# Gated recurrence of a two-block model: scaling at the last level, one rate product for both directions, and where the keys' factor is applied

## The reference

```
q = silu(q_raw);  v = i_in
f = lb + (1 - lb) * sigmoid(f_raw)         # for both directions: (256, 2, 1024)
log_f = log(max(f, 1e-30))
k = (1 - lb) * sigmoid(-f_raw)
o_f = scan(q, k[0], v, log_f[0])           # state = state * f_t + k_t v_t;  o_t = q_t . state
o_b = flip(scan(flip(q), flip(k[1]), flip(v), flip(log_f[1])))
y_hg = group_rmsnorm(o_f + o_b) * silu(g_out)
```

## Time and profile before

| | |
|---|---|
| median of 3 runs | 2481.41 us (2479.23 to 2483.37) |
| profiled execution, its own time | 2486.97 us |
| its span | 2485.1 us |
| PE busy | 2430.2 us, 98% |
| DVE busy | 1787.8 us, 72% |
| ACT busy | 1451.0 us, 58% |
| POOL busy | 287.6 us, 12% |
| mean granted clock of TensorE | 0.995 of full |

### The profile page before, as it was taken

One profiled execution on the slowest core, in us unless ns is written; L12 is line 12 of the kernel. 1 busy time (PEld: TensorE's weight loads), 2 busy tenths in 40 slices (PEclk: granted clock), 3 DMA queues, 4 the chain that ended last, 5 costly groups with the idle time before them and its releaser, 6 DMA issues.

```text
span 2485.1 us, 43110 instructions
## 1 busy us (share of the span) xinstructions
PE 2430.2 (98%) x17744; PEld 2225.9 (90%) x17744; DVE 1787.8 (72%) x2889; ACT 1451.0 (58%) x2130; POOL 287.6 (12%) x222
## 2 busy tenths in 40 slices
PE   8999999999999999899999999999999999999998
PEld 7888999888889899798999799998898999899996
DVE  4558675565586755589778897885599768887875
ACT  5547555545475555477656655664767656556654
POOL 0000002000000000002124710000012207500000
PEclk9999999999999999999999999999999999999999
DMA  7554476655545556554567646565554557645663
GB/s 246 160 141 125 154 253 192 203 181 167 141 119 153 185 189 204 166 159 123 154 189 200 198 134 194 184 190 190 145 159 137 172 173 205 181 151 186 190 209 127
DMA packets 358921, 430.50 MB, mean 173 GB/s; under 512 B 20617, under 2 KB 286311, under 8 KB 358469
## 3 DMA queue, kind: packets, MB, share of 16 engines
q1 hardware_dynamic: 341312, 401.72, 52.9%
q10 hardware_dynamic: 14340, 14.93, 2.7%
q0 software_dynamic: 3072, 11.10, 1.5%
HBM read 424.44 MB, written 3.24 MB: 172 GB/s over the span
## 4 chain that ended last, share of the span: by engine, by line
PE 86%; DVE 10%; ACT 2%; issue 1%; DMA 1%; ACTq 0%; POOL 0%; POOLq 0%; DVEq 0%
PE ps L112 84%; DVE wlo L121 3%; PE ps L115 2%; DVE sE L121 1%; DVE hgA L148 1%; DVE hgQF L121 0%; ACT L118 0%; DVE hgQB L121 0%; ACT lnv L118 0%; DVE hgkf L121 0%; DVE hgkb L121 0%; DMA kT<-in_diff_lambda 0%; DVE sbc L130 0%; DVE sE L124 0%; ACT whi L118 0%
## 5 line engine op out<-in xcount | busy, mean ns | idle before, releaser
L121 DVE TENSOR_TENSOR wlo<-wring,whi 128x1024 fp32r<-128x1024 f32 (+1 forms) x768 | 919.8, 1218 | 252.5 <-ACT whi L118 252.2
L118 ACT ACTIVATE whi<-wring 128x1024 fp32r<-128x1024 f32 (+1 forms) x768 | 803.4, 1054 | 428.3 <-PE ps L112 416.0
L112 PE MATMUL ps<-uT,whi 128*128 128x256 f32 x4640 | 821.7, 281 | 6.0 <-DVE wlo L121 4.7
L112 PEld LDWEIGHTS ps<-uT,whi 128*128 128x128 f32 x4640 | 706.4, 188 | 16.3 <-DVE wlo L121 8.1
L112 PE MATMUL ps<-uT,wlo 128*128 128x256 f32 x2320 | 646.8, 279 | 0.0
L112 PEld LDWEIGHTS ps<-uT,wlo 128*128 128x128 f32 x2320 | 437.5, 189 | 0.0
L112 PE MATMUL ps<-xT,whi 128*128 128x256 f32 x2112 | 375.0, 282 | 2.3 <-DVE xT L121 1.1
L112 PEld LDWEIGHTS ps<-xT,whi 128*128 128x128 f32 x2112 | 320.3, 187 | 9.4 <-issue 5.2
L112 PE MATMUL ps<-xT,wlo 128*128 128x256 f32 x1056 | 293.7, 278 | 0.0
L112 PE MATMUL ps<-whi,hid 128*128 128x512 f32 x864 | 269.5, 391 | 0.0
L112 PEld LDWEIGHTS ps<-xT,wlo 128*128 128x128 f32 x1056 | 197.8, 187 | 0.3
(11 more groups left out here) (400 smaller groups left out, 3565.4 us busy)
## 6 DMA issues: line engine op xcount, KB each, us to landing
wring<-in_w_in SPq DMA_DIRECT2D x346, 512.0 KB, 4.2
wring<-in_mlp_w SPq DMA_DIRECT2D x128, 512.0 KB, 4.5
wring<-in_w_up SPq DMA_DIRECT2D x88, 512.0 KB, 4.6
wring<-in_w_down SPq DMA_DIRECT2D x44, 512.0 KB, 4.3
wring<-in_w_branch SPq DMA_DIRECT2D x32, 512.0 KB, 3.4
wring<-in_w_out SPq DMA_DIRECT2D x32, 512.0 KB, 4.3
wring<-in_mem_w_kv SPq DMA_DIRECT2D x16, 512.0 KB, 6.4
wring<-in_w_br_hg SPq DMA_DIRECT2D x16, 512.0 KB, 4.7
```

The costliest lines, as they stand in the source:

```text
L112: return self.e.matmul(*p, **k) if self.e else Nothing()
L118: return self.e.activation(*p, **k) if self.e else Nothing()
L121: return self.e.tensor_tensor(*p, **k) if self.e else Nothing()
```

## The change

`hg_scale` at level 6 works only on the tokens that `hg_cross` reads: 4 instructions of 256 columns in place of 512. The four rate buffers become one tile `W.T` in which both directions lie 768 columns apart, and f and b become two parts of one 2048-column tile `hgfb`, so that one instruction makes both directions' rates at levels 0 to 5, and `hg_split` is one instruction of 2048 columns in place of two of 1024. In `forget_scale` the maximum is one instruction of 512 columns in place of two of 256, and the two multiplications of the keys move to a new ScalarE part of the same step: two activations of 256 columns with a per-channel scale, in place. `hg_start` and level 0's merge now wait for ScalarE's signal for the keys, and `hg_split` for the maxima.

```diff
@@ -1030,9 +1030,10 @@
                 return out
-            B.f, B.kf = ar.take("hgf", 1024, at=o + 1024), ar.take("hgkf", 1024, at=o + 3072)
+            B.fb, B.kf = ar.take("hgfb", 2048, at=o + 1024), ar.take("hgkf", 1024, at=o + 3072)
+            B.f, B.b = B.fb.part("f", 0, 1024), B.fb.part("b", 1024, 1024)
             yield from projB(w, GF + c0, 512, uT, forget(B.f, B.kf, hf * 4))
-            B.b, B.kb = ar.take("hgb", 1024, at=o + 2048), ar.take("hgkb", 1024, at=o + 4096)
+            B.kb = ar.take("hgkb", 1024, at=o + 4096)
             yield from projB(w, GF + 1024 + c0, 512, uT, forget(B.b, B.kb, 8 + hf * 4))
@@ -1065,9 +1066,9 @@
             do("hg_cross", B, [AB.take(), AB.take()])
-            ar.give(B.q, B.f, B.b, B.kf, B.kb)
+            ar.give(B.q, B.fb, B.kf, B.kb)
             if hf:
-                ar.give(*W.Tf, *W.Tb, *W.QK[1])
+                ar.give(W.T, *W.QK[1])
             yield
@@ -1101,9 +1102,9 @@
             W = Box()
-            W.QF, W.QB, W.At = ar.take("hgQF", 1024, at=8192), ar.take("hgQB", 1024, at=9216), ar.take("hgA", 2048, at=10240)
-            W.Tf = [ar.take("hgTf", 512, at=12288), ar.take("hgTf", 256, at=12800)]
-            W.Tb = [ar.take("hgTb", 512, at=13056), ar.take("hgTb", 256, at=13568)]
+            W.Q2, W.At = ar.take("hgQ", 2048, at=8192), ar.take("hgA", 2048, at=10240)
+            W.QF, W.QB = W.Q2.part("F", 0, 1024), W.Q2.part("B", 1024, 1024)
+            W.T = ar.take("hgT", 1536, at=12288)
             W.QK = [[ar.take("hgQm", 1024, at=13824 + 2048 * i), ar.take("hgKm", 1024, at=14848 + 2048 * i)] for i in range(2)]
@@ -1270,7 +1271,7 @@
             yield from branch(acc, a["w_br_hg_2"][l], 0, yT, gT[1], 0, keep=True)
-            ar.give(gT[1], W.QF, W.QB, W.At)
+            ar.give(gT[1], W.Q2, W.At)
         weave((ssd_proj(), 1), (hg_branch(), 1))
@@ -1951,6 +1952,14 @@
 
+    def forget_scale(c, fk, kk, i0, k):
+        e.wait_ge(*at("bounds"))
+        e.wait_ge(*at((kk.name, "sig", k)))
+        for j in range(2):
+            v = kk.ap[:, (k + j) * 256:(k + j + 1) * 256]
+            o = e.activation(v, v, ACT.Copy, scale=K.oms[:, c.l, i0 + k + j:i0 + k + j + 1])
+        o.then_inc(*up("act_forget", (kk.name, k)))
+
     def halves(x, side, n):
...
@@ -2518,18 +2527,13 @@
         e.wait_ge(*at((fk.name, "sig", k)))
-        fs, ks = ([x.ap[:, (k + j) * 256:(k + j + 1) * 256] for j in range(2)] for x in (fk, kk))
+        fs = fk.ap[:, k * 256:k * 256 + 512]
         lb, om = ([v[:, c.l, i0 + k + j:i0 + k + j + 1] for j in range(2)] for v in (K.lbs, K.oms))
         for j in range(2):
-            o = e.tensor_scalar(fs[j], fs[j], om[j], lb[j], ALU.mult, ALU.add)
+            o = e.tensor_scalar(fs[:, j * 256:j * 256 + 256], fs[:, j * 256:j * 256 + 256], om[j], lb[j], ALU.mult, ALU.add)
         o.then_inc(*up("dve_forget"))
         e.wait_ge(*now("dve_forget"))
-        for j in range(2):
-            e.tensor_scalar(fs[j], fs[j], TINY, None, ALU.max)
-        e.wait_ge(*at((kk.name, "sig", k)))
-        for j in range(2):
-            o = e.tensor_scalar(ks[j], ks[j], om[j], None, ALU.mult)
-        o.then_inc(*up("dve_forget", (kk.name, k)))
+        e.tensor_scalar(fs, fs, TINY, None, ALU.max).then_inc(*up("dve_forget", (fk.name, k)))
 
@@ -2554,23 +2558,34 @@
             e.wait_ge(*at((B.q.name, k)))
-        e.tensor_tensor(W.QF.ap, B.q.ap, B.f.ap, ALU.mult)
-        e.tensor_tensor(W.QB.ap, B.q.ap, B.b.ap, ALU.mult).then_inc(*up("dve_hg", ("hgsplit", B.tag)))
+        for x in (B.f, B.b):
+            e.wait_ge(*at((x.name, 2)))
+        both = lambda x: x.ap.rearrange("p (d n) -> p d n", d=2)
+        e.tensor_tensor(both(W.Q2), B.q.ap.rearrange("p (d n) -> p d n", d=1).to_broadcast([128, 2, 1024]), both(B.fb), ALU.mult).then_inc(
+            *up("dve_hg", ("hgsplit", B.tag)))
 
...
         nb = 1024 // (2 * n)
-        half = lambda x, side: x.ap.rearrange("p (n c s) -> p n c s", c=2, s=n)[:, :, side, :]
-        Tf, Tb = (B.f, B.b) if j == 0 else (W.Tf[(j - 1) % 2], W.Tb[(j - 1) % 2])
-        tp = lambda x, side: x.ap[:, 0:1024 // n].rearrange("p (n c) -> p n c", c=2)[:, :, side]
-        tb = lambda x, side: x.ap[:, 0:1024 // n].rearrange("p (n c) -> p n c", c=2)[:, :, side:side + 1].to_broadcast([128, nb, n])
+        T2 = B.fb.ap.rearrange("p (d n) -> p d n", d=2) if j == 0 else rates(W, j - 1)
+        if j < 6:
+            half = lambda x, side, own: x.ap.rearrange("p (n c s) -> p n c s", c=2, s=n)[:, :, side, :]
+            rate = lambda d, side, own: T2[:, d, :].rearrange("p (n c) -> p n c", c=2)[:, :, side:side + 1].to_broadcast([128, nb, n])
+        else:
+            half = lambda x, side, own: x.ap.rearrange("p (h b c s) -> p h b c s", h=4, b=2, c=2)[:, :, own, side, :]
+            rate = lambda d, side, own: T2[:, d, :].rearrange("p (h b c) -> p h b c", h=4, b=2)[:, :, own, side:side + 1].to_broadcast([128, 4, 64])
         e.wait_ge(*now("dve_hg"))
-        for x, side, T, ev, name in ((W.QF, 1, Tf, "hgQF", "QF"), (B.kf, 0, Tf, "hgK", "kf"), (W.QB, 0, Tb, "hgQB", "QB"), (B.kb, 1, Tb, "hgK", "kb")):
+        for x, side, own, d, ev, name in ((W.QF, 1, 1, 0, "hgQF", "QF"), (B.kf, 0, 0, 0, "hgK", "kf"), (W.QB, 0, 0, 1, "hgQB", "QB"), (B.kb, 1, 1, 1, "hgK", "kb")):
             e.wait_ge(*at((ev, B.tag, j)))
-            e.tensor_tensor(half(x, side), half(x, side), tb(T, 1 - side), ALU.mult).then_inc(*up("dve_hg", ("hgscaled", B.tag, j, name)))
+            v = half(x, side, own)
+            e.tensor_tensor(v, v, rate(d, 1 - side, own), ALU.mult).then_inc(*up("dve_hg", ("hgscaled", B.tag, j, name)))
         if j < 6:
-            e.tensor_tensor(W.Tf[j % 2].ap[:, 0:nb], tp(Tf, 0), tp(Tf, 1), ALU.mult)
-            e.tensor_tensor(W.Tb[j % 2].ap[:, 0:nb], tp(Tb, 0), tp(Tb, 1), ALU.mult).then_inc(*up("dve_hg"))
+            t4 = T2.rearrange("p d (n c) -> p d n c", c=2)
+            e.tensor_tensor(rates(W, j), t4[:, :, :, 0], t4[:, :, :, 1], ALU.mult).then_inc(*up("dve_hg"))
+
+    def rates(W, j):
+        o = 512 * (j % 2)
+        return W.T.ap.rearrange("p (d n) -> p d n", d=2)[:, :, o:o + (512 >> j)]
 
```

More of the change, by code:

```diff
@@ L2112, in scalar_program @@
                  merged=merged, ln_stats=ln_stats, ln_out=ln_out, relu_square=relu_square, square_part=square_part, square_rows=square_rows, rms_scale=rms_scale, small_gates=small_gates,
-                 cumsum_rows=cumsum_rows, store_rows=store_rows, store_max=store_max, spread_rows=spread_rows, ml_max_cols=ml_max_cols, forget_out=forget_out, hg_merge=hg_merge, hg_first=hg_first, hg_cross=hg_cross,
+                 cumsum_rows=cumsum_rows, store_rows=store_rows, store_max=store_max, spread_rows=spread_rows, ml_max_cols=ml_max_cols, forget_out=forget_out, forget_scale=forget_scale, hg_merge=hg_merge, hg_first=hg_first, hg_cross=hg_cross,
                  hg_values=hg_values, hg_norm=hg_norm, ssd_conv=ssd_conv, ssd_silu=ssd_silu, ssd_turn=ssd_turn,
```

## The result

The changed kernel takes 2474.82 us (median of 20 executions, 2471.25 to 2480.16) against 2481.23 for the kernel before in the same session (20 executions, 2477.14 to 2486.78). The ratio is 0.9975, 95% interval 0.9969 to 0.9982: 6.2 us faster, between 4.5 and 7.7. The forecast was 5.4 us and 2476.0.

A forecast was written before the change was run, and what follows sets the result against it. TensorE, busy 98%, bounds the kernel; edits pay only in its 5.87 us of waits for VectorE in half 0's scans. Taking 2.7 us in each layer, 5.4 us, from 2481.41 gives 2476.0 us; range 2473.8 to 2481.0.

The forecast's parts named there:

- The place: Half 0's scans: TensorE starts level 5's products 1.07 us and the crossing 1.78 us late; ceiling 5.87 us over both layers.
- The sum: VectorE reaches half 0's crossing 2.75 us earlier a layer: 0.07 + 6 x 0.07 + 2 x 0.59 + 1.08.
- six rate products: Levels 0 to 5 on VectorE: one rate instruction fewer at each level, saving 0.07 us each.
- two forget_scale: Two gate steps before the crossing: keys leave VectorE and maxima become one instruction, saving 0.59 us each.
- three such delays: GpSimd's copy holds up the first rate product at levels 0, 4 and 5, about 0.45 us each; left in the forecast.
- Level 5's products: TensorE's matmuls at level 5 in half 0's scan: 0.94 us of their 1.07 us lateness goes.
- the prediction's own sign of being wrong: Half 0's scan: level 5's products or the crossing still over 0.5 us late would count against the forecast.
- forecast slack of 1.4 us: ScalarE's last merge copy before level 6, with the keys' pair in front, ends 1.4 us before level 6's products.
- Slower: Rival: ScalarE falls behind through table loads, 3.4 us a pair, starving TensorE for wlo; 7.8 us slower, 2489.2; chance 0.09.
- threshold of 0.9 us a pair: Half 0's projection: from this price on, two ScalarE pairs use up its 1.8 us idle and eat into the lead.
- Hidden anyway: Rival: TensorE reaches a later wait 2.7 us earlier and waits there for something self-paced; near 2481; chance 0.11.
- Half of it: Rival: GpSimd's copy also delays rate products at levels 1 to 3, costing 1.35 us; 2.8 us gained, 2478.6; chance 0.28.

The follow-up runs named there:

- e5: Changed kernel with masked copies into hgA at levels 1 to 3 done for one head of four; ratio to before 0.9975 (0.9957 to 0.9994).
- a0: Changed kernel run again with no edit; ratio to before 0.9996 (0.9979 to 1.0013).
- e8: Kernel before with only GpSimd's merge copy of QB into Qm moved to ScalarE; ratio to before 0.9989 (0.9977 to 1.0000).
- a1: Changed kernel run a third time with no edit; ratio to before 0.9985 (0.9974 to 0.9995).
- e2: Kernel before with only the new forget_scale (keys on ScalarE, maxima in one instruction); ratio to before 0.9988 (0.9976 to 0.9999).
- e6: Changed kernel with two more pairs of plain in-place copies behind each ScalarE pair of the keys; ratio to before 1.0008 (0.9990 to 1.0027).
- e3: Changed kernel with level 6 whole, two maxima and keys on VectorE, leaving joint rate product and hg_split; ratio to before 1.0001 (0.9988 to 1.0014).
- e4: Changed kernel with the keys back on VectorE, all else kept; ratio to before 0.9990 (0.9977 to 1.0004).
- e7b: Repeat of e7, changed kernel with GpSimd's merge copy of QB on ScalarE; 2474.13 us, ratio to before 0.9978 (0.9967 to 0.9989).
- b0: Kernel before run once more against itself with no edit; ratio 1.0009 (1.0000 to 1.0018).
- e7: Changed kernel with GpSimd's merge copy of QB into Qm done by ScalarE; 2480.16 us, ratio to before 0.9966 (0.9950 to 0.9982).

## Why the prediction was right

**The place.** The prediction named two late starts of TensorE in half 0's scan and 5.87 us as all there is to gain. The hgkb wait is gone, 0.5 us of the hgKm wait is left, and e5 confirms the ceiling from the other side. Of 5.87 us, 5.18 went; on the repeated profiles (5.90 before, 0.77 and 0.94 after) about as much. That the median came within 1.2 us of the forecast is partly luck, since repeats of this comparison differ by more than that; that about 5 us of idle time in two scans went is not.

**The sum.** 2.75 us a layer at the crossing; D fell by 2.90 and 2.79. Term by term, by the distances between starts in the first layer:

| term | forecast | measured |
|---|---|---|
| hg_split | 0.07 | 0.07 |
| six rate products | 0.42 | 0.57 |
| two forget_scale | 1.18 | 1.17 |
| level 6 | 1.08 | 1.07 |

The rate terms of levels 0 to 3 came out at 0.06 to 0.07 each. Those of levels 4 and 5 are 0.10 and 0.20, because the copy's hold at level 5 fell on a tensor_scalar with 0.3 in place of 0.45; in the second layer it fell on the rate product again, and the six sum to 0.45. That levels 4 and 5 would keep their hold, and levels 1 to 3 stay free, was right for this kernel in five layers of six (in a0's second, level 4 is free), but for a weaker reason than I gave. The forecast also counted three such delays and missed a fourth, on the wlo splits behind hg_split, which take 2.81 us with GpSimd's copy beside them and 2.35 in e8: with all of them gone VectorE's lead grows by 1.85 us and not by the 1.35 of its bound.

**Level 5's products.** 0.94 earlier was forecast; counted from the scan's start they are 0.91 earlier (35.92 for 36.83) in both layers. The second layer's wait is 0.17, near the 0.13 of the sum. The first layer's is 0.51, and 0.53 and 0.50 in a1 and a0. By the prediction's own sign of being wrong (over 0.5 us late) that is just past the line, and 0.52 us of idle time is just over the 0.5 that it had set for right. The missing 0.34 us lies at the scan's entry: VectorE's hgKm starts 0.45 us behind the instruction in front of it, where it was 0.11, with 0.26 of idle time for which the profile names no releaser. Before, then changed, first layer:

```profile
1101.64 0.19 DVE L121 TENSOR_TENSOR sm<-ps,sm 128x32 f32<-128x32 f32 x1 [3.46 <-PE ps L115]
1101.75 1.22 DVE L121 TENSOR_TENSOR hgKm<-hgkf,hgkb 128x1024 f32<-128x1024 f32 x1
...
1101.07 0.19 DVE L121 TENSOR_TENSOR sm<-ps,sm 128x32 f32<-128x32 f32 x1 [3.46 <-PE ps L115]
1101.52 1.23 DVE L121 TENSOR_TENSOR hgKm<-hgkf,hgkb 128x1024 f32<-128x1024 f32 x1 [0.26 <-issue]
```

The gap stands in the first layer of all eight profiles in which the keys are scaled on ScalarE (0.24 to 0.26 us), and in none of the six in which VectorE scales them; no second layer has it. So it comes with the keys' move, in which `hg_start` waits for ScalarE's signal, and this is a term that the forecast put at nothing and that cost something: 2.49 us of the first layer's idle time went for 2.69 of the second's. It is not the keys coming late, since ScalarE has them done 19 us before (1082.06). Why the first layer alone has it stays open.

**ScalarE.** 0.80 us a pair, as taken, without a table load. The forecast slack of 1.4 us at level 6's merge is 1.66. "ScalarE: Activation LUTs" of the Trainium skill (Rules for kernel authors) would have kept the multiplication on VectorE; price and rule agree (0.80 for 0.52), and e2, in which keys and joint maximum together took 2.4 us of idle time away, shows that the move pays all the same.

**The rivals.** *Slower* was wrong in its price (no loads) and in its place: e6 shows that ScalarE's lateness reaches TensorE first through the small gates and not through wlo or the merge. Its threshold of 0.9 us a pair was close to the 1.1 that e6 gives, by luck, since it was worked out from another limit. What held was its caution: beyond the room, e6 paid more than the theory allowed. *Hidden anyway* did not happen: the crossing's lead arrives at the end of the span. *Half of it* did not happen in this kernel, but its mechanism is real: e3 and e4 have it in their second layer, for 1.23 and 1.25 us, where the forecast priced it at 1.35, and e5 has it in part in both layers. My argument against it (the same three levels in both layers, the same instruction in front of each rate product) was too weak, since e3 keeps that instruction too. "SBUF — State Buffer" in the Trainium skill (Who interferes with whom) gives GpSimd and VectorE one shared port pair as an exclusive lock, which goes to whoever issues first. e7b agrees with the lock, since the four delays vanish with GpSimd's copy; e3, where one list goes both ways, shows that the order in the list does not tell who is first.

**The rest of the 6.2.** 5.2 us are the scans. The other 1.0 lies within the interval of 4.5 to 7.7, and waits elsewhere differ by as much between executions of one kernel: a wait of TensorE for xT is 1.1 us in the profile of the kernel before and in a1, and 1.7 in b0 and a0, and one of 1.9 for memT stands in the kernel before alone. No cause is needed for it, and none was shown. The other comparisons (3.7 and 1.0 us) do not contain it.

## What to carry to other kernels

Where the bounding engine is 98% busy, price an edit by the late starts that it can move, and look for the ceiling there first: here it was 5.87 us, three parts shared it, and the fourth (GpSimd's copy) found most of it taken and paid the rest back in the next scan. Look behind the stretch too: a window with no idle time can have pushed its wait 4 us on. A costlier instruction on an engine that is idle at that point beats a cheap one on the engine that is waited for; make it longer to find out where it would start to cost. When the effect is a few tenths of a per cent, compare idle times and distances between fixed instructions of the trace beside the medians.

## What the runs showed of the hardware

**TensorE runs the same matmuls at two paces, at full granted clock.** The feed-forward of a layer has a run of 1248 matmuls without a wait. Chain of the kernel before, both layers:

```profile
1542.38 168.05 PE ps L112 x1248
...
2269.46 163.50 PE ps L112 x1248
```

The identical kernel b0, both layers:

```profile
1541.59 163.50 PE ps L112 x1248
...
2262.62 168.06 PE ps L112 x1248
```

The changed kernel takes 163.5 us in both layers. One layer of a profile is at times slower by 4.55 us: the first in the kernel before and in e5, the second in b0, a0 and e7; neither in any other profile, the changed kernel's first and a1 among them. The clock row shows 1.00 in both, and the mean of a 256-column matmul is 281 ns against 276. So 4.55 us between the two profiled spans are chance; other stretches gave 1.4 of it back, which leaves the 3.1 us of busy time in the 10.1. Over all profiles TensorE's busy time went from 2422.4 to 2433.7 us for the same work. What sets the pace stays open.

**Which engine waits in a collision of GpSimd's copy with VectorE is settled neither by the instructions nor by their widths.** The price is 0.41 to 0.47 us when a VectorE product is the one held up, 0.3 for a tensor_scalar, nothing when it is the copy (1.56 to 2.42 us in place of 0.95). It can differ between two layers of one execution (e3, e4) and between two executions of one kernel (level 4 of the second layer: 0.63 us in the changed kernel's first profile, 0.22 in a0).
